# Expert weights over two DMA queues: the down matrices from ScalarE's queue, gate and up matrices from SP's

## The reference, cut to what matters

```
D_MODEL, SEQ, N_EXPERTS, EXPERT_DIM, TOP_K = 1024, 512, 64, 256, 8
scores = sigmoid(t @ w_router)            # t: 512 x 1024, all f32
idx    = the 8 best experts of a token    # by score and bias, within 4 of 8 groups
g   = einsum('td,edf->tef', tb, w_eg)     # gate, 1024 x 256 per expert
u   = einsum('td,edf->tef', tb, w_eu)     # up,   1024 x 256 per expert
act = silu(g) * u * gates
out = einsum('tef,efd->td', act, w_ed)    # down, 256 x 1024 per expert
```

## Time and profile before

| | |
|---|---|
| median of three runs | 2017.49 us |
| the profiled execution: time, span | 2020.52 us, 2018.5 us |
| TensorE (PE) busy | 1642.4 us, 81% of the span |
| VectorE (DVE) busy | 1328.2 us, 66% |
| ScalarE (ACT) busy | 930.2 us, 46% |
| SP's DMA queue q1 | 295.19 MB, 39.6% of the 16 DMA engines' span |
| GpSimd's queue q0 | 45.29 MB, 6.1% |
| ScalarE's queue q10 | 19.78 MB, 2.5% |

### The profile page before, as it was taken

How to read it: one execution, slowest core, us unless ns; L and a number is a source line. 1 busy time by engine, 2 the same in 40 slices (tenths; PEclk the granted TensorE clock), 3 DMA queues, 4 the chain that set the end, 5 groups by cost and what they waited for, 6 DMA issues and landing times.

```text
span 2018.5 us, 22744 instructions
## 1 busy us (share of the span) xinstructions
PE 1642.4 (81%) x7242; PEld 1277.6 (63%) x7243; DVE 1328.2 (66%) x1717; ACT 930.2 (46%) x1132; POOL 293.8 (15%) x282
## 2 busy tenths in 40 slices
PE   6697797699789798698797473999999789999960
PEld 1484685588567476486586352778777567877740
DVE  2486467546755647756635674878888557988849
ACT  2225424432233233223323313778888457888840
POOL 1000000000200200201010035122222222222210
PEclk9698799799889799798798686999999889999985
DMA  8210120136033033042061106889999667999948
GB/s 260 83 63 22 50 97 22 63 110 224 0 111 119 0 125 104 14 144 72 21 222 47 42 1 247 324 328 380 367 366 379 232 244 295 379 364 357 345 175 362
DMA packets 107634, 361.43 MB, mean 179 GB/s; under 512 B 19116, under 2 KB 29552, under 8 KB 80528
## 3 DMA queue, kind: packets, MB, share of 16 engines
q1 hardware_dynamic: 79920, 295.19, 39.6%
q0 software_dynamic: 22688, 45.29, 6.1%
q10 hardware_dynamic: 4928, 19.78, 2.5%
HBM read 352.18 MB, written 43.66 MB: 196 GB/s over the span
## 4 chain that ended last, share of the span: by engine, by line
PE 63%; DVE 13%; DMA 12%; ACT 5%; issue 4%; POOL 2%; ACTq 1%; SPq 0%; POOLq 0%; DVEq 0%
PE psum L1209 17%; PE psum L1211 16%; PE psum L1210 16%; DMA rawm<-in_w_exp_up 6%; DMA rawm<-in_w_exp_down 3%; DVE ring L802 2%; PE psum L1409 2%; POOL slot_table L494 2%; PE psum L643 2%; PE psum L1231 2%; DVE ofin L885 1%; ACT ring L730 1%; PE psum L1389 1%; PE psum L1363 1%; PE psum L1335 1%
## 5 line engine op out<-in xcount | busy, mean ns | idle before, releaser
L802 DVE TENSOR_TENSOR ring<-rawm,ring 128x2048 fp32r<-128x2048 f32 x192 | 436.3, 2287 | 39.5 <-ACT ring L730 39.0
L730 ACT ACTIVATE ring<-rawm 128x2048 fp32r<-128x2048 f32 x192 | 368.2, 1919 | 90.3 <-DMA rawm<-in_w_exp_up 40.5
L1209 PE MATMUL psum<-ring,xT 128*128 128x512 f32 x528 | 225.6, 427 | 28.2 <-DVE ring L802 23.0
L1506 DVE TENSOR_TENSOR hl<-raw,hl 128x2048 fp32r<-128x2048 f32 x59 | 134.4, 2291 | 144.9 <-ACT hl L1017 144.5
L1211 PE MATMUL psum<-ring,xT 128*128 128x512 f32 x528 | 212.0, 401 | 0.0
L1210 PE MATMUL psum<-ring,xT 128*128 128x512 f32 x528 | 211.6, 401 | 0.0
L1209 PE MATMUL psum<-hl,hT 128*128 128x512 f32 x416 | 165.5, 398 | 11.2 <-DVE hT L1783 11.2
L1017 ACT ACTIVATE hl<-raw 128x2048 fp32r<-128x2048 f32 x59 | 112.0, 1911 | 130.2 <-PE psum L1211 94.7
L589 POOL DMA_INDIRECT y_rows<-yb,row_of x64 | 99.6, 1556 | 440.4 <-ACT yb L774 431.7
L1211 PE MATMUL psum<-hl,hT 128*128 128x512 f32 x416 | 163.3, 393 | 0.0
L1210 PE MATMUL psum<-hl,hT 128*128 128x512 f32 x416 | 163.3, 393 | 0.0
(11 more groups left out here) (370 smaller groups left out, 3052.3 us busy)
## 6 DMA issues: line engine op xcount, KB each, us to landing
rawm<-in_w_exp_gate SPq DMA_DIRECT2D x64, 1024.0 KB
rawm<-in_w_exp_up SPq DMA_DIRECT2D x64, 1024.0 KB
rawm<-in_w_exp_down SPq DMA_DIRECT2D x64, 1024.0 KB
raw<-in_w_in SPq DMA_DIRECT2D x36, 1024.0 KB, 5.1
raw<-in_w_ada SPq DMA_DIRECT2D x24, 1024.0 KB, 5.3
ysum<-y_rows ACTq DMA_DIRECT2D x16, 1024.0 KB, 9.0
raw<-in_w_branch_b SPq DMA_DIRECT2D x8, 1024.0 KB, 5.3
raw<-in_w_branch_a SPq DMA_DIRECT2D x4, 1024.0 KB, 5.2
```

Of the source, the lines that this page charges most:

```text
L730: A(ring[:, slot, 1, :], rawm[slot][:], ACT.Copy).then_inc(S["m_hi2"], 1)
L802: TT(ring[:, slot, 0, :], rawm[slot][:], ring[:, slot, 1, :].bitcast(F32), ALU.subtract).then_inc(S["m_lo2"], 1)
L1209: M(dst, lhs(0), rhs(0), start=first, stop=False)
L1506: TT(h_[:, 1, :], r, h_[:, 0, :].bitcast(F32), ALU.subtract).then_inc(S["lo_done"], 1)
```

## The change

SP's `load` issues only gate and up of an expert (the first three experts are as before). ScalarE gets a function `load_down`, called at the head of its `it(e)`, ahead of the wait for `xt_ps` and the copy of the tokens. It issues the down matrix of e+1 on ScalarE's queue. It has no wait of its own: the wait for `dn_ps` >= e-1, ahead of the copy to `yb` in `it(e-1)`, stands before it in ScalarE's program. SP's wait for `dn_ps` is gone.

```diff
             def load(e, par, first=False):
                 at = bass.ds(e, 1)
-                for u in range(3):
+                for u in range(3 if first else 2):
                     slot = 3 * par + u
                     if not first:
-                        if u < 2:
-                            sp.wait_ge(S["xt_ps"], e)
-                        else:
-                            sp.wait_ge(S["dn_ps"], e - 2)
+                        sp.wait_ge(S["xt_ps"], e)
...
+            down = w_exp_down[0].rearrange("e (p k) n -> e p k n", p=P)
+
+            def load_down(e, par):
+
+                slot = 3 * par + 2
+                a.dma_start(rawm[slot].rearrange("p (k n) -> p k n", n=D),
+                            down[bass.ds(e, 1)].rearrange("o p k n -> (o p) k n")).then_inc(S[f"m_raw{slot}"], 16)
+
             def it(e, par, turn, two):
...
                 prev, nxt = (par + 2) % 3, (par + 1) % 3
+                if more_ and (not isinstance(e, int) or e >= 2):
+                    load_down(e + 1, nxt)
                 if more_:
                     a.wait_ge(S["xt_ps"], e + 2)
                     x_hi(nxt).then_inc(S["xt_hi"], 1)
```

## The result

The changed kernel takes 2094.24 us (median of four runs, 2092.16 to 2100.42), against 2017.26 us before. The ratio is 1.0393, with a 95% interval of 1.0358 to 1.0428. It is slower by 77 us, where 35 us were forecast, so the sign was right and the size less than half. The time lies inside both ranges that were given, 2035 to 2095 and 2000 to 2105, at their upper ends. The profiled execution has a span of 2098.5 us.

What follows compares the result with a forecast made beforehand. Transfers were taken to bound 40 of 63 cycles, TensorE about 14; a 10.5 us loop would add 12 + 8 + 9 + 6 = 35 us, giving 2053 us (58%), own range 2035 to 2095, 8-in-10 range 2000 to 2105.

Steps and rivals of the forecast that it cites:

- The bound of the kernel before: Expert stage: transfers bound 40 of 63 cycles (9.97 us in the long stretch), TensorE about 14 (9.43 us).
- The moment of the issue: On ScalarE: down issued 2.3 to 3.2 us later, behind next gate and up and behind its own earlier split.
- The second part of the loop, 1.9 us: On ScalarE, start of down split to next down issue: between 0.9 and 2.73 us, the split alone taken.
- The landing, 8.6 us: Down issue to landing: 5.1 us alone, 2.8 for alternating with SP's queue, 0.7 for gathers and scatters.
- half of the rows' 1.5 us: Within the landing: gathers and scatters, 0.56 MB, delay the down matrix up to 1.5 us; 0.7 us taken.
- The upper end of 12.2 us: Landing if the down matrix is served behind both gate and up: 5.1 + 2 x 2.8 + 1.5 us.
- The cycle, 10.5 us: Expert stage: longest of TensorE 9.43, transfers 9.97 (10.02) and loop 8.6 + 1.9 = 10.5 us.
- The sum: Added time in the expert stage: long stretch 12, last 8, fast 9, other cycles 6; 35 us in all.
- The issue on ScalarE, cost at nothing: Each cycle's 0.43 us issue is hidden by ScalarE's down wait; uncovered, 61 x 0.43 = 26 us.
- No change: Rival, 20%: the down matrix lands in time and transfers still set the cycle; 2017 to 2021 us.
- Faster: Rival, 14%: two queues move more than one, cycles fall to TensorE's 9.43 us; 1995 us.
- Far slower: Rival, 8%: down served after next gate and up, 14.1 us a cycle; 2247 us, or half that loss.

Runs made afterwards that it cites:

- before_no_gather: The kernel before, with gathers that move hardly a row (row index bound 0): 1979.13 us, ratio 0.9805.
- spread: The kernel before, with the first 64 tokens of an expert placed on the even partitions, the rest on the odd: 1985.25 us, ratio 0.9848.
- early: The changed kernel, with ScalarE issuing the down matrix of e+2 right behind the dn_ps wait, ahead of the reads of the counts: 2025.84 us, ratio 1.0028.
- hold: The changed kernel, with SP's gate and up waiting for xt_hi in place of xt_ps, so issued behind the down matrix: 2039.37 us, ratio 1.0104.
- loop_last: The kernel before, SP alone issuing gate and up of e+2 first, then down of e+1 after the copy to yb (y_ev): 2112.59 us, ratio 1.0474.
- late: The kernel before, SP alone issuing gate and up of e+2 first, then down of e+1, keeping the dn_ps wait: 2120.39 us, ratio 1.0514.
- loop_first: The kernel before, one queue in the old order, but the down issue waits for the copy to yb (y_ev) instead of dn_ps: 2025.37 us, ratio 1.0036.
- probe: The kernel before, with ScalarE also issuing an 8 KB DMA into a spare buffer once a cycle, 61 times: 2023.64 us, ratio 1.0027.
- swap: The kernel before, with gate and up issued on ScalarE's queue and down kept on SP's: 2032.43 us, ratio 1.0077.
- ahead: The changed kernel, with the down matrix of e+2 issued before the split of the down matrix of e+1: 2032.69 us, ratio 1.0073.

## Why the prediction was right in its sign and wrong in its size

**The bound of the kernel before.** Right. Transfers set the 9.97 us and TensorE the 9.43: before_no_gather brings the mean of these cycles to 9.4. What "transfers" meant was too coarse, a mean share of 0.96 at 372 GB/s. With the same bytes the spread kernel moves 391 GB/s: a few DMA engines were late with their part of each load (4.3 us behind the median), and they set the cycle.

**The moment of the issue.** Right: behind the copy to yb, behind the next gate and up, and in a loop with its own split.

**The second part of the loop, 1.9 us.** The number was right, 1.8 us in the timeline, with a mean of 2.07 us, as in some cycles the copy to yb waits for TensorE. The reason was wrong, so this is luck. The split does not have to end before the issue; what takes the time is that ScalarE reads the counts between (L512 in the chain), which the prediction left out. The early kernel shows what this was worth: 0.8 in place of 2.07 us.

**The landing, 8.6 us.** This is the step that failed: "With SP's queue taking turns with ScalarE's, one for one" plus half of the rows' 1.5 us. The mean was 9.2 us, 9.5 us in the long stretch, and the page's median 9.7 us. The upper end of 12.2 us was wrong too.

The turns one for one did not come about. The packets of the 23 loads of the long stretch show this: the first packet of a down matrix comes 3.3 us after its issue (2.3 to 3.9 us), and by then SP's queue has moved 1.24 MB, more than half of gate and up. Beside the packets of the down matrix it moves only 0.4 MB more, and the gathers and scatters 0.3 MB. In 21 of the 23 cycles the up matrix lands before the down matrix. In hold, where the down matrix is issued 1.9 us ahead of gate, its first packet comes 1.2 us after the issue. So what the down matrix lost was a late start behind SP's two loads, not every second turn. Why its packets wait for these loads was not tried.

By the moment of the gate issue the picture is simple. In the changed kernel down is issued 2.1 us behind gate and lands at 2.1 + 9.2 = 11.3 us; in loop_last, one queue, at 3.4 + 8.6 = 12.0; in late at 1.0 + 10.6 = 11.6. Whichever is last of three lands some 11 to 12 us after the first issue, on one queue or two. From the earlier trace rows, 5.1 + 2 x 2.8 + 0.7 = 11.4 us, less the 2.1 us of head start is 9.3 us. I should have summed the line and taken off the head start. This sum was made after the result, and it is an estimate: in the long stretch, with 2.5 us of head start, it gives 8.9 us for the 9.5 measured. The rows had a nearer value as well, which the prediction names and does not use: the down matrix itself, first in its line, was split 10.4 us after its issue.

What the sharing of the engines does is to make up land later, 10.0 us against 7.7 us in loop_last by their pages, and down hardly sooner. That agrees with the Trainium skill, "DMA: Bandwidth & Descriptors", section "Queues, rings and completion order", so far as that queues share the DMA engines; it is no reason for a short landing when the other queue holds two loads.

**The cycle, 10.5 us.** For the 23 cycles of the long stretch (means, us; "wait" is from the landing to the start of the split, "second part" from there to the next down issue):

| kernel | landing | wait | second part | cycle |
|---|---|---|---|---|
| before | 9.87 | 0.04 | 0.05 | 9.97 |
| changed | 9.50 | 0.02 | 2.06 | 11.65 |
| early | 9.80 | 0.13 | 0.36 | 10.20 |
| hold | 8.11 | 0.05 | 2.16 | 10.25 |
| loop_first | 7.45 | 0.07 | 2.86 | 10.27 |
| loop_last | 8.50 | 0.02 | 2.96 | 11.53 |

The three parts follow one another in time, so they add up to a cycle in any kernel, with or without a loop, and that they do so proves nothing. What shows the loop in the changed kernel is that the split starts 0.02 us after the landing, that the next issue stands behind this split in ScalarE's program (in the kernel before it does not), and the edits that mainly change one part: early takes 1.7 us off the second part and the cycle loses 1.45, hold takes 1.4 off the landing and the cycle loses 1.4. Against the kernel before, the landing did not get longer (9.87 to 9.50 us); what was added are the 2 us between split and issue. So the loop was the right frame. In this stretch its two terms were 0.9 and 0.2 us too small. A loop 0.5 us over the bound was forecast, and 1.7 us came: where two bounds lie close, a small error in one doubles the loss.

**The sum.** Long stretch 39 for 12 us, last 19 for 8, fast 14.5 for 9, the rest 7 for 6.

**The issue on ScalarE, cost at nothing.** Nearly right. The probe has 5 us (2 to 9) for 61 issues, not 26.

**The rivals.** "No change" needed a short landing, which did not come. "Faster" did not come: the rate fell to 321 GB/s in the long stretch, and no kernel with the same rows and two queues passed the 372 GB/s of before (early 363, hold 362, swap 365, ahead 361). "Far slower" had the order that came, down last of the three, and the wrong price: 12.2 us counts the whole line from the down issue, and by then a part of it has been served, so that 9.2 us came.

**What stays open.** Why a down matrix has no packet for 3.3 us behind two loads on the other queue. In the changed kernel the last of the 16 increments of a down matrix comes 1.7 us behind the median one in the long stretch, and with spread rows still 1.4 us, so rows explain little of it there, though in the kernel before they explain more than half (4.3 to 1.9 us). The pairing of short and long cycles was not tried.

## What to carry to other kernels

In this kernel the order of need counted, and one queue written in that order gave it for nothing; no kernel with weights on two queues was faster than the kernel before, and the one with down behind gate and up was the slowest of them. Before moving a load to an engine that also computes, write down the loop issue, landing, work on what landed, next issue, with the landing as the whole line of pending loads less the head start; if it comes near the cycle, put the issue ahead of everything the engine need not do first. And look at whether rows of an indirect transfer lie on a part of the partitions only.

## What the runs showed of the hardware that was not expected

- Spreading the valid rows of gathers and scatters from the first 64 partitions to the even ones raised the rate from 372 to 391 GB/s with the same bytes, and took 33 us off the kernel before. With that, the wait for weights in the long stretch is nearly gone.
- A DMA share of 0.96 at 372 GB/s was not the most that these engines move: the share was a mean over engines of which a few were late. Taking the gathers out (0.30 MB of 3.71 MB a cycle, 8%) took 38 us off, and the last increment of a down matrix then came 1.3 us behind the median one, not 4.3 us.
- A load on ScalarE's idle queue, issued 2.5 us behind two loads on SP's, had its first packet 3.3 us after its issue; issued 1.9 us ahead of them (hold), 1.2 us.
- A DMA issue between ScalarE's activations cost 0.09 us net in the probe (5 us over 61 issues, 0.04 to 0.14 us each by the interval), a quarter of the 0.34 us that the issue takes in the timeline.
